# Triangular solve on packed blocks of 32 and 64, q left unnormalised, and half tiles of a branch product between the solve's levels

## The reference, cut to what matters

```
q = l2_norm(q) * (DN_HEAD_K ** -0.5)      # 8 heads of 128; eps 1e-6
k = l2_norm(k)
M = where(strict, (k*beta) @ k.T * decay, 0)
sol = triangular_solve(I + M, rhs)        # u, w
o = q_dec @ state + a_qk @ v_new
o = o * rsqrt(mean(o*o) + EPS) * norm_w * silu(z)
merged = sigmoid(gate_s) * (y_s @ ssm_w_branch) + sigmoid(gate_d) * (y_d @ dn_w_branch)
```

## Time and profile before

| | us |
|---|---|
| median of 3 runs | 3296.53 |
| lowest and highest | 3293.74, 3297.16 |
| span of the profiled execution | 3296.9 |
| TensorE busy | 3258.3 |
| VectorE busy | 2306.1 |
| ScalarE busy | 646.3 |
| GpSimd busy | 283.7 |

### The profile page before, as it was taken

How to read it: one execution, slowest core, us unless ns; L and a number is a source line. 1 busy time by engine, 2 the same in 40 slices (tenths; PEclk the granted TensorE clock), 3 DMA queues, 4 the chain that set the end, 5 groups by cost and what they waited for, 6 DMA issues and landing times.

```text
span 3296.9 us, 57970 instructions
## 1 busy us (share of the span) xinstructions
PE 3258.3 (99%) x24390; PEld 3071.0 (93%) x24390; DVE 2306.1 (70%) x5141; ACT 646.3 (20%) x1455; POOL 283.7 (9%) x348
## 2 busy tenths in 40 slices
PE   9999999999999999999999999999999999999998
PEld 8999888899999998888999999979999999889998
DVE  5657575477666575754776698877687798867785
ACT  1113233221111132331211101202211111212211
POOL 0202000000102020001001000200012000200031
PEclk9999999999999999999999999999999999999999
DMA  5444344244545443433454444344344454343443
GB/s 199 167 154 141 128 141 137 84 155 169 173 162 172 156 141 128 144 130 104 165 169 164 154 167 168 129 153 155 127 167 167 163 171 167 119 150 128 161 172 129
DMA packets 85412, 497.01 MB, mean 151 GB/s; under 512 B 20864, under 2 KB 25376, under 8 KB 26144
## 3 DMA queue, kind: packets, MB, share of 16 engines
q1 hardware_dynamic: 71840, 490.63, 43.6%
q10 hardware_dynamic: 13312, 2.67, 0.4%
HBM read 491.16 MB, written 2.11 MB: 150 GB/s over the span
## 4 chain that ended last, share of the span: by engine, by line
PE 88%; DVE 8%; DMA 1%; ACT 1%; issue 1%; ACTq 0%; SPq 0%; DVEq 0%
PE bank L340 81%; DVE xT L857 1%; PE bank L1948 1%; DVE arena L989 1%; DVE arena L987 1%; DVE arena L991 1%; DVE arena L1476 1%; PE bank L498 1%; DVE arena L1731 1%; DVE arena L1728 0%; DVE arena L986 0%; PE bank L2677 0%; PE bank L2013 0%; PE bank L2620 0%; PE bank L2020 0%
## 5 line engine op out<-in xcount | busy, mean ns | idle before, releaser
L340 PE MATMUL bank<-arena 128*128 128x128 f32 x8640 | 1021.8, 275 | 2.4 <-DVE arena L991 2.3
L340 PEld LDWEIGHTS bank<-arena 128*128 128x128 f32 x8640 | 992.6, 192 | 3.1 <-DVE arena L991 3.1
L340 PE MATMUL bank<-arena,ring 128*128 128x128 f32 (+1 forms) x6080 | 957.7, 311 | 6.1 <-DMA ring<-w 6.1
L340 PEld LDWEIGHTS bank<-arena,ring 128*128 128x128 f32 x6080 | 866.5, 192 | 67.9 <-issue 16.5
L340 PE MATMUL bank<-xT,ring 128*128 128x128 f32 (+1 forms) x5440 | 859.6, 313 | 4.5 <-DVE xT L857 2.8
L340 PEld LDWEIGHTS bank<-xT,ring 128*128 128x128 f32 x5440 | 777.4, 191 | 57.3 <-DVE xT L857 4.8
L986 DVE TENSOR_TENSOR arena<-ring 128x512 f32<-128x512 f32 x318 | 218.8, 688 | 131.1 <-PE bank L340 112.8
L942 ACT ACTIVATE arena<-bank 128x128 f32<-128x128 f32 x286 | 79.2, 277 | 1093.4 <-PE bank L340 1088.3
L1040 DVE TENSOR_TENSOR arena<-arena,bank 128x256 f32<-128x256 f32 x286 | 119.2, 417 | 203.1 <-ACT arena L942 202.3
L340 PE MATMUL bank<-xT,arena 128*128 128x128 f32 x1728 | 229.1, 276 | 2.8 <-DVE arena L991 2.7
L991 DVE TENSOR_TENSOR arena<-ring,arena 128x512 f32<-128x512 f32 x318 | 223.1, 702 | 11.0
(11 more groups left out here) (305 smaller groups left out, 2369.1 us busy)
## 6 DMA issues: line engine op xcount, KB each, us to landing
ring<-w SPq DMA_DIRECT2D x461, 1024.0 KB, 4.9
hT<-hT_d SPq DMA_DIRECT2D x4, 256.0 KB, 4.7
ring<-w SPq DMA_DIRECT2D x4, 256.0 KB, 5.1
arena<-blocks_d ACTq DMA_DIRECT2D x4, 256.0 KB, 6.8
arena<-memT_d SPq DMA_DIRECT2D x1, 1024.0 KB, 7.8
outT<-hT SPq DMA_DIRECT2D x4, 256.0 KB, 2.4
cst<-cst_d SPq DMA_DIRECT2D x1, 860.5 KB, 9.1
arena<-dmask_d SPq DMA_DIRECT2D x1, 768.0 KB, 9.2
```

Of the source, the lines that this page charges most:

```text
L340: ins = self.e.matmul(out, lhsT, rhs, start=start, stop=stop)
```

## The change

The q half of step 1 is dropped: only k is normalised, with four sums and three halves between them, and one after. Since o is linear in q, o is computed from raw q; ScalarE squares q once more with a factor, VectorE adds that to the squares of o ahead of the sum (a new wait of TensorE, `o_squared`), and the sum's guard becomes P * EPS * EPS.

The solve works on the blocks alone. The inverted 32 x 32 blocks are loaded twice by ScalarE's queue: packed into `diag_t` (`base_loaded`), then into the diagonal of `inv_t` (`diag_loaded`). VectorE turns `diag_t` into `diag` with one transposing copy within 32 x 32 blocks. Level 32 is 32 matmuls of 32 x 32 by 32 columns (`at32`), 16 (`x32`) and 32 (`tat32`); level 64 is 16 matmuls of 64 x 64 by 64 columns (`at64`) and 16 (`tat64`). The masks and the turns go. Halves are set after `at32`, before `tat64` and after it, and one more ahead of the solve, in place of the four that left step 1. The weights are packed in the new order.

```
-        spec += many(L, "branch_s", 4, "dve") + many(L, "gate_d", 4, "act") + ... + many(L, "branch_s", 4, "dve", 4)
+        spec += many(L, "branch_s", 2, "dve") + many(L, "gate_d", 4, "act") + ... + many(L, "branch_s", 6, "dve", 2)
# first_act
+    for i in range(4):
+        e.activation(m.q_sq[:, i], m.qkv[:, 2 * i:2 * i + 2, :], ACT.Square, scale=P * EPS ** 0.5).then_inc(sems.squares_ready, 1)
     e.preload_act_table_set(EXP_TANH)
...
     e.wait_ge(sems.base_stored, 32 * (L + 1))
+    e.wait_ge(sems.chain_done, CHAIN.filled(L, "kv_rows", 3))
+    for b in range(BLOCKS):
+        e.dma_start(m.diag_t[b * BASE:(b + 1) * BASE], by_unit(m.base_d)[:, b].rearrange("u i j -> i u j")).then_inc(sems.base_loaded, 16)
     for b in range(BLOCKS):
-        e.dma_start(block(m.inv_t, b), ...).then_inc(sems.base_loaded, 16)
+        e.dma_start(block(m.inv_t, b), ...).then_inc(sems.diag_loaded, 16)
...
+    negated("x32", 0, m.inv64[BASE:2 * BASE, :, 0:BASE], slice(BASE, 2 * BASE), BASE)
+    for i in range(2):
+        negated("tat32", i, units(m.inv_t)[low, :, high], low, BASE)
+    for i in range(2):
+        negated("tat64", i, units(m.inv_t)[0:HALF_P, 8 * i:8 * i + 8, HALF_P:P], slice(0, HALF_P), HALF_P)
# first_dve
+    e.wait_ge(sems.base_loaded, 16 * BLOCKS * (L + 1))
+    e.transpose(m.diag..., m.diag_t...).then_inc(sems.diag_turned, 1)
+    # two multiplications by beta for at32, branch_s(3), two for at64, branch_s(4), branch_s(5)
+    for i in range(4):
+        e.wait_ge(sems.squares_ready, upto(L, "squares_ready", SSM_GROUPS + 8 + i + 1))
+        tt(x, x, m.q_sq[:, i], ALU.add).then_inc(sems.o_squared, 1)
# first_pool
-            e.tensor_tensor(dst, units(m.nT, q), mask..., ALU.mult).then_inc(sems.parts_ready, 1)
+    e.memset(m.inv64[0:BASE, :, BASE:2 * BASE], 0.0)
+    e.wait_ge(sems.diag_turned, upto(L, "diag_turned", 1))
+    e.tensor_copy(m.inv64[0:BASE, :, 0:BASE], m.diag[0:BASE])
+    e.tensor_copy(m.inv64[BASE:2 * BASE, :, BASE:2 * BASE], m.diag[BASE:2 * BASE]).then_inc(sems.diag_ready, 1)
# first_pe
-    for i in range(8):
+    for i in range(4):
...
     beside()
-    e.wait_ge(sems.base_loaded, 16 * BLOCKS * (L + 1))
+    beside()
+    e.wait_ge(sems.diag_turned, upto(L, "diag_turned", 1))
+    banks = [t.open_chain(L, "at32", i) for i in range(2)]
+    for u in range(UNITS):
+        for i in range(2):
+            low, high = piece(2 * i), piece(2 * i + 1)
+            ins = e.matmul(banks[i][high, piece(u)], nT[low, u, high], m.diag[low, u, :], start=True, stop=True)
+    beside()
+    e.wait_ge(sems.chain_read_dve, CHAIN.read(L, "at32", 0))
+    for u in range(UNITS):
+        ins = e.matmul(bank[high, piece(u)], m.diag_t[high, u, :], m.ax32[high, u, :], start=True, stop=True)   # x32
+    # tat32 in the form of at32, with ax32 and diag_t
+    e.wait_ge(sems.chain_read_act, CHAIN.read(L, "x32", 0))
+    # at64: nT[low, u, high] with inv64[low, u, :]
+    e.wait_ge(sems.chain_read_act, CHAIN.read(L, "tat32", 1))
+    e.wait_ge(sems.diag_loaded, 16 * BLOCKS * (L + 1))
+    beside()
+    # tat64: waits for the read of at64; ax64[high, u, :] with inv_t[high, u, high]
+    beside()
+    e.wait_ge(sems.chain_read_act, CHAIN.read(L, "tat64", 1))
```

More of the change, by code:

```diff
@@ L196, in __init__ @@
         self.normed = sem("normed")
+        self.o_squared = sem("o_squared")
         self.eg_ready = sem("eg_ready")
@@ L599, in chain_jobs @@
                 spec += [((L, "y_norm", p // 4 - 1), "act")]
-        spec += many(L, "qk_norm", 8, "act") + many(L, "g_seg", 4, "dve") + many(L, "kk", 4, "dve") + many(L, "kq", 4, "dve")
+        spec += many(L, "k_norm", 4, "act") + many(L, "g_seg", 4, "dve") + many(L, "kk", 4, "dve") + many(L, "kq", 4, "dve")
         spec += many(L, "kv_rows", 8, "dve")
[L602 to L610, removed]
+        spec += many(L, "at32", 2, "dve") + [((L, "x32", 0), "act")] + many(L, "tat32", 2, "act")
+        spec += many(L, "at64", 2, "dve") + many(L, "tat64", 2, "act")
         spec += many(L, "u0", 2, "act") + many(L, "wt", 2, "act") + many(L, "state", 2, "act") + many(L, "v1", 2, "act")
@@ new lines, in first_dve @@
+    branch_s(3)
+    for i in range(2):
+        some = slice(8 * i, 8 * i + 8)
+        e.wait_ge(sems.chain_done, CHAIN.filled(L, "at64", i))
+        tt(m.ax64[HALF_P:P, some], bk[CHAIN.bank(L, "at64", i)][HALF_P:P, :].rearrange("p (u n) -> p u n", n=HALF_P),
+           beta[HALF_P:P, some].unsqueeze(2).to_broadcast([HALF_P, 8, HALF_P]), ALU.mult).then_inc(sems.chain_read_dve, 1)
+    branch_s(4)
+    branch_s(5)
+    for i in range(4):
+        x = m.sq_d[:, i, :].rearrange("p (t n) -> p t n", n=S)
+        e.wait_ge(sems.squares_ready, upto(L, "squares_ready", SSM_GROUPS + 8 + i + 1))
+        tt(x, x, m.q_sq[:, i], ALU.add).then_inc(sems.o_squared, 1)
+        seen.up("o_squared")
@@ L1817, in first_pool @@
         weights_by_pool(g, m.seven_xbc, ring, FAST_FROM[L, "xbc_7"] + i)
[L1818 to L1832, removed]
+    e.wait_ge(sems.chain_done, CHAIN.filled(L, "kv_rows", 3))
+    e.memset(m.inv64[0:BASE, :, BASE:2 * BASE], 0.0)
+    e.wait_ge(sems.diag_turned, upto(L, "diag_turned", 1))
+    e.tensor_copy(m.inv64[0:BASE, :, 0:BASE], m.diag[0:BASE])
+    e.tensor_copy(m.inv64[BASE:2 * BASE, :, BASE:2 * BASE], m.diag[BASE:2 * BASE]).then_inc(sems.diag_ready, 1)
+    seen.up("diag_ready")
     feed_by_pool(g, m, L, "ffn2")
@@ L1943, in beside, with norm_sums @@
         t.part((L, "branch_s", i), m.xbc, 2 * KD, half)
-    def norm_sums(name, i, squares, first):
+    def norm_sums(name, i, squares):
         bank = t.open_chain(L, name, i)
-        e.wait_ge(sems.squares_ready, upto(L, "squares_ready", first + i + 1))
         e.matmul(bank[:, :], const("ones"), squares, start=True, stop=True).then_inc(sems.chain_done, 1)
-    for i in range(8):
+    for i in range(4):
         if i == 1:
@@ L1982, in first_pe @@
     flat = lambda x: x.rearrange("p h t n -> p (h t) n")
[L1983 to L1992, removed]
+    inv_t, nT = flat(m.inv_t), flat(m.nT)
     for i in range(4):
@@ new lines, in first_pe @@
+    beside()
+    bank = t.open_chain(L, "x32", 0)
+    low, high = piece(0), piece(1)
+    e.wait_ge(sems.chain_read_dve, CHAIN.read(L, "at32", 0))
+    for u in range(UNITS):
+        ins = e.matmul(bank[high, piece(u)], m.diag_t[high, u, :], m.ax32[high, u, :], start=True, stop=True)
+    ins.then_inc(sems.chain_done, 1)
+    banks = [t.open_chain(L, "tat32", i) for i in range(2)]
+    e.wait_ge(sems.chain_read_dve, CHAIN.read(L, "at32", 1))
+    for u in range(UNITS):
+        for i in range(2):
+            low, high = piece(2 * i), piece(2 * i + 1)
+            ins = e.matmul(banks[i][low, piece(u)], m.ax32[high, u, :], m.diag_t[high, u, :], start=True, stop=True)
+            if u == UNITS - 1:
+                ins.then_inc(sems.chain_done, 1)
@@ new lines, in first_pe @@
+    low, high = slice(0, HALF_P), slice(HALF_P, P)
+    e.wait_ge(sems.chain_read_act, CHAIN.read(L, "x32", 0))
+    for i in range(2):
+        bank = t.open_chain(L, "at64", i)
+        for j in range(8):
+            u = 8 * i + j
+            ins = e.matmul(bank[high, j * HALF_P:(j + 1) * HALF_P], nT[low, u, high], m.inv64[low, u, :], start=True, stop=True)
+        ins.then_inc(sems.chain_done, 1)
+    e.wait_ge(sems.chain_read_act, CHAIN.read(L, "tat32", 1))
+    e.wait_ge(sems.diag_loaded, 16 * BLOCKS * (L + 1))
@@ L2027, in heads @@
+    beside()
+    for i in range(2):
+        bank = t.open_chain(L, "tat64", i)
+        e.wait_ge(sems.chain_read_dve, CHAIN.read(L, "at64", i))
+        for j in range(8):
+            u = 8 * i + j
+            ins = e.matmul(bank[low, j * HALF_P:(j + 1) * HALF_P], m.ax64[high, u, :], inv_t[high, u, high], start=True, stop=True)
+        ins.then_inc(sems.chain_done, 1)
+    beside()
+    e.wait_ge(sems.chain_read_act, CHAIN.read(L, "tat64", 1))
     def heads(name, f):
@@ L2059, in first_pe @@
     for i in range(4):
-        norm_sums("o_norm", i, m.sq_d[:, i, :], SSM_GROUPS + 8)
+        e.wait_ge(sems.o_squared, upto(L, "o_squared", i + 1))
+        norm_sums("o_norm", i, m.sq_d[:, i, :])
     beside()
```

124 lines of the change are left out of this document (53 added, 71 removed).

## The result

| | before | after |
|---|---|---|
| median, us | 3296.85 (4 runs, 3293.74 to 3298.66) | 3262.47 (4 runs, 3261.44 to 3264.32) |
| span of the profiled execution | 3296.9 | 3259.6 |
| TensorE busy | 3258.3 | 3226.6 |

The ratio is 0.9895, with an interval of 0.9883 to 0.9908: 34.4 us faster, where 28.5 were forecast. The profiled execution of after took 3261.44, 1.8 above its span.

What follows compares the result with a forecast made beforehand. TensorE, busy 3258.3 of 3296.9 us, was taken to bound the kernel. Removed work, small matmuls, starts behind waits and idle summed to -51.15 + 20.5 + 1.0 + 0.3 = -29.4, forecast 3268 us, range 3258 to 3284.

Steps and rivals of the forecast that it cites:

- What goes: TensorE, step 1 and solve: four sums a layer, the old solves and the idle ahead of them go, together 51.15 us.
- What comes: TensorE, new solve: small matmuls at 0.040 us a narrow record and 0.060 a wider one, 20.5 us in both layers.
- The turned blocks: Ahead of at32: blocks land at 609.0, copy takes 0.7 us; idle 0.3 in layer 0, none in layer 1.
- The cover: In the solve: halves and small matmuls hide other engines' reads; uncovered, each place costs about 1 us, four in two layers 4.
- place called tightest: Between tat32 and at64: ScalarE's reads of tat32 stay covered by at64, with 0.4 us to spare.
- The clock falls: Rival, in the solve: small matmuls lower TensorE's clock; 3271 to 3274 with one or two stretches a layer, all 3290; chance 0.15.
- Fixed pace: Rival, in the solve: each small record costs 0.070 us, 31.4 instead of 20.5 in all, giving 3279; chance 0.15.
- waits that stay open: Rival, at the solve: copy at 2.5 us, layer 0's clock drop and tight places show, giving 3276; chance 0.1.
- no overlap: Rival, in the solve: small records keep the full tiles' pace, 51.1 us, giving 3298, no change; chance 0.04.
- a drain at each position: Rival, at32 and tat32: the array drains at each change of position, 79.5 us instead of 20.5, giving 3326; chance 0.04.
- The norm of q: Rival, ahead of o's norm: q's squares and additions hold up o's first sum, costing 4 x 0.6 a layer; chance 0.01.
- The base: Whole kernel: forecast starts from the profiled execution's 3296.9 us, whose span is 0.4 above the median of 3296.53.

Runs made afterwards that it cites:

- halves ahead: The changed kernel with its three halves between the solve's levels issued before at32 instead: 3274.78 us, ratio 0.9928 to the kernel before.
- the solve alone: The kernel before with only the new block solve, q normalised and halves placed as before, none between the levels: 3288.67 us, ratio 0.9972.
- by position: The changed kernel with at32 and tat32 going through all units at one array position, then all at the other: 3271.94 us, ratio 0.9922.
- one half ahead: The changed kernel with only the half before tat64 moved ahead of at32: 3265.83 us, ratio 0.9905 to the kernel before.
- at32 sixteen times: The changed kernel with at32's same products issued 16 times over in each layer: 3319.94 us, ratio 1.0067 to the kernel before.

## Why the prediction was right, step by step

- **What goes: right.** Step 1 from its first sum to `g_seg` took 34.50 us and takes 17.25: 17.25 sooner, 17.2 forecast. The idle ahead of at32 is gone.
- **What comes: mis-sized.** The terms were 20.5 for the records, 1.0 for starts behind waits and 0.3 of idle, 21.8 in all. From at32 to the heads after takes 36.09 us in two layers, less six halves at 3.45: 15.4. A layer holds 64 records in 1.13, 96 in 2.04 and 64 in 4.01 us. A record of at32 or tat32 costs 0.018 us, one of x32, whose neighbours share a position, 0.031 (29 in 597.10 to 598.01), a 64-wide one 0.063; taken were 0.040, 0.040 and 0.060. Together 14.4. The mistake lay in choosing 0.040 between 0.026 and 0.114: the earlier trace rows showed 0.026 for loads of 64 columns, and half of that width went below it. Starts behind waits cost nothing that can be seen; instead a half next to small matmuls takes 3.65 (3.56 ahead of the heads) and not 3.45, 0.5 a layer, 1.0 in all.
- **The turned blocks: right in the copy, wrong in the landing.** The copy takes 0.70, as taken. The chain ahead of it got shorter: from the load's issue to VectorE's start of the substitution it was 7.9 us in layer 0 (the earlier trace rows has the end of it) and is 4.7; for the inverses, from the store's issue to that of the loads, 6.6 and is 4.3 (3.8 in layer 1). The loads of the inverses are issued 7.0 us sooner after `g_seg` than before. I had taken the round trips through DRAM as they were; why they got shorter no run shows. Wrong too was that VectorE's branch column ahead of the copy is done long before: it ends as the copy starts, in both layers, so that blocks landing still sooner would gain nothing. The four squares of q on ScalarE did not move the multiplications by the decay: these end 12.3 us after `g_seg` starts in both kernels, where 0.4 later was forecast.
- **The cover: right where the halves stand; the clock was missing from its price.** In after no reader is late. The place called tightest (tat32's reads) was not it: with x32 and tat32 over so soon, x32's reader had 1.04 us instead of 2.6, just enough. Four uncovered places were priced at 4 us; without the halves two waits a layer cost 3.1 (halves ahead), and a third, ahead of at32, another 3.5 (the solve alone). The clock costs another 9 to 10.
- **The clock falls: absent in after, but a real rival.** With the halves in place it stays away, without them it falls in both layers. I had priced a fall at 1.5 us for one stretch and at up to 11 us a layer, with 0.15; the experiments show 9 us in two layers without the halves, and a fall worth 3.2 us in one layer where nothing but the order of narrow records had changed.
- **Fixed pace, waits that stay open, no overlap, a drain at each position: refuted.** All would show in the 18.04 us. The last is the wrong way round: alternating positions is the faster order, 0.018 against 0.032 at one position (by position: 2.04/64). Its threshold of 0.16 us a record comes to 0.15 when the sum is redone; nothing hangs on it.
- **The norm of q: right.** The additions end 1.3 us before the first sum of o.
- **The base.** I set the profiled execution's time equal to its span. If it lay 1.8 above, as after's does, the start was 1.8 too low; the fourth run of before, 3298.66, which wasn't known then, lies just there. That this error went against the one in the records is luck: it hides 1.8 us of it. The sum forecast -29.4 between the spans; with 6.4 less of new work, 0.1 between this count and that from the first sum, and the 1.4 from untouched stages it is the -37.3 that were found. These are two single executions; between the medians it is 34.4.

Why the clock fell in layer 1 of the by-position kernel and not in its layer 0, nor with one half ahead, stays open. Narrow matmuls are common to all falls but that of the earlier trace rows, which followed an idle; the halves ahead and the solve alone had waits of 0.86 us as well. Where in a kernel the clock fell was read in one execution each; of the other runs only the mean clock is known. No run moved a single half from behind at32, so which of the three matters most was not measured.

## What to carry to other kernels

Small matmuls cost little: 0.018 us a record of 32 x 32 when neighbours lie in different parts of the array, 0.032 in the same part, 0.063 for 64 x 64 in the same part, against 0.11 for a full tile. So a block structure is worth spelling out. Leave wide matmuls between them: here they covered 3.1 us of hand-overs, and with them in place TensorE stayed at 2.4 GHz, which was worth 9 more. Before adding up edits measured alone, ask whether one gives the other its cover; here 9.1 and 11.4 us made 33 to 34.

## What the runs showed of the hardware

- A busy TensorE can lose its clock. In the by-position kernel it was busy 4.00 of 4 us in each window and fell to 0.50; in at32 sixteen times it was busy 12.00 of 12 us in layer 1 and stayed at 0.50. The Trainium skill (TensorE: Matmul & The Clock Gate, "Part 1: The HAM clock gate (the "warmup" mystery)") says that activity releases the throttle. These rows show TensorE busy at 1.2 GHz all the same while its matmuls were narrow, and at 2.4 GHz again after one half of wide ones.
- Narrow records start 0.018 us apart in after and 0.016 in the first 256 of at32 sixteen times, 0.026 at the lower clock (156 in 4 us); at one position they start 0.032 apart (by position). The Trainium skill (TensorE: Matmul & The Clock Gate, "Wait — 56ns, not 53.3ns?") has about 25 ns as the least; by the measurement it is lower where neighbours differ in position.
